# Attention scores in one VectorE pass, heads in pairs on partition halves, and filler products in the norm waits

## The chip, the cores and the metric

The kernel runs on one core of a Trainium2 chip. The metric is the device time of one execution in microseconds, the median of several runs. Five engines work side by side and meet only at semaphores: TensorE (PE; its weight loads are listed as PEld), VectorE (DVE), ScalarE (ACT), GpSimd (POOL) and SyncE (SP), which issues the weight loads.

## The reference

Two transformer blocks on 512 tokens of width 1024, all in float32. The first has two layers: SwiGLU feed-forward, a mixer, another feed-forward, each behind a residual and a layer norm, then `h + (p @ w_proj) * sigmoid(h @ w_gate)`. The mixer of layer 0 is a short convolution beside a state-space model. That of layer 1 is an attention of 8 heads of width 128 over 2 key heads, in which every query sees the 128 best keys by an index score. The second block is an RMS norm, an attention with 8 heads in three branches and 8 sliding-window heads with sinks, and a mixture of experts. What the change touches is the scores and their softmax:

```python
# compressed, selected and window branch; slopes are those of ALiBi, d = 64
s = einsum(q, k) * d ** -0.5
s = s - slope * dist
p = masked_softmax(s, mask)          # row maximum, exp, sum, divide
o = g0 * (p_cmp @ v) + g1 * (p_slc @ v) + g2 * (p_win @ v)
# sliding heads: window 128, the sink takes part in the maximum and in the sum
m = maximum(max(s), sink); z = sum(exp(s - m)) + exp(sink - m)
```

The norms are `(x - mean) * rsqrt(var + eps) * g + b` and `x * rsqrt(mean(x * x) + eps) * g`, over the 1024 features, which lie on the partitions in 8 chunks.

## The kernel before

Activations lie transposed, features on the partitions and 512 tokens in the free dimension. Weights come through a ring of six blocks of 1 MB that SyncE fills in the order of use. TensorE's results go into eight PSUM banks. A planner (`g`, class `Groups`) hands them out at build time: `hold` or `add` gives a label the next bank in turn (or the one named), and with it what must have been read before TensorE may write there. The order of work on each engine is written out by hand in one program per engine, and every engine works in order.

**Attention.** Class `Attention` serves both attentions as a list of items. An item is one head and one block `b` of 128 queries (b = 0 to 3). In the first attention (`att_c`, head width 128) an item has one branch with (b+1) x 128 keys. In the second (`att_n`, head width 64) tiles 0 to 3 have three branches: compressed (31 keys), window (128, 256, 384, 384 keys) and selected (128, 256, 384, 512); the first two share a bank, group 0, the third is group 1. Tiles 4 to 7 have one sliding branch (128, 256, 256, 256). A tile holds two heads, `kv` 0 on partitions 0 to 63 and `kv` 1 on 64 to 127; all four blocks of one are done, then those of the other. Both have 32 items per part: 32, and 32 + 32.

The items pass through a pipeline written out per step i:

- TensorE: scores of item i+1 (L1634), transposes of the weighted probabilities of i-2 (L1644, recorded under the helper's line L505), values times probabilities of i-3 (L1656, into half a bank at head width 64).
- VectorE: for item i the sum of the scores and the distances per branch (L1691, or L1693 with the slope), a maximum per branch (L1701), for sinks L1704, then the negated maximum (L1706); for item i-1 the factor 1/z (L1712 or L1714, L1716, and L1720 times the branch gate); for i-2 the copy of the transposes out of PSUM, when (group + item) is odd (L1671).
- ScalarE: exponentials with row sums for i (L1736), the other copies of i-2 (L1673), and after block 3 the head's output (L1893, L2115).
- POOL: probabilities times factor, one pass per branch (L1752).

Scores and transposes take turns on banks 0 to 5, outputs on 6 and 7. A matmul in float32 is recorded as two passes (two MATMUL and two LDWEIGHTS records), a transpose as one.

**Norms.** `tensor_stats` folds the sums and the squares of the chunks onto few partitions (L578), then spreads the mean to all (L585); VectorE makes the variance, ScalarE the root, VectorE the reciprocal (L650), and `tensor_scales` spreads that (L585 again). VectorE then subtracts and multiplies chunk by chunk (L631, L657), ScalarE applies gain and bias (L668), and the next product starts with the first chunk. In the norms "ffn1" and "ffn3" eight projections stand beside this (L469), four between the two spreads, four behind the second, and then the gate's products (L478); their banks are the next eight in turn, so that of projection 6 is the one of the spread mean. ScalarE copies projections 0 to 3 before its eight norm steps and 4 to 7 behind them (L1078).

## Time and profile before

| | us |
|---|---|
| median of 3 runs | 3364.46 (3362.58 to 3366.96) |
| the profiled execution | 3364.31 |
| its span in the trace | 3362.5 |
| TensorE busy | 3136.2 (93%) |
| VectorE busy | 1392.2 (41%) |
| ScalarE busy | 471.0 (14%) |
| POOL busy | 316.2 (9%) |
| mean granted clock of TensorE | 0.963 |

The page gives the busy time of each engine and the chain of work that ended last, followed back from the last instruction. The trace behind it can be asked by window, by line and in order of time. Matmuls are pipelined, so their durations overlap; the time from start to start tells more. A granted clock of 1.00 is TensorE's 2.4 GHz level, 0.50 its 1.2 GHz level. Line numbers are those of the kernel before.

### The profile page before, as it was taken

The numbers are of one execution on the slowest core, as the hardware profiler recorded it, in microseconds if no ns is written. First come the engines' busy times: TensorE is split into PE (matmuls) and PEld (weight loads), VectorE is DVE, ScalarE is ACT, GpSimd is POOL, SyncE is SP. The second block draws the span as 40 slices with busy tenths as digits, with TensorE's granted clock in tenths as the row PEclk, the third lists the DMA queues.
The fourth block names the chain that finished last, engine by engine and source line by source line (L and its number), as shares of the span: only waits on it lengthen the run. The fifth ranks groups of instructions, "written<-read, shape, count | busy, mean of one in ns | idle before, by whom it ended". The sixth has DMA issues, their size and how long they took to land.

```text
span 3362.5 us, 31721 instructions
## 1 busy us (share of the span) xinstructions
PE 3136.2 (93%) x12846; PEld 2170.7 (65%) x12846; DVE 1392.2 (41%) x3041; ACT 471.0 (14%) x1020; POOL 316.2 (9%) x304
## 2 busy tenths in 40 slices
PE   9999999889999999999997999999899989997774
PEld 7886446738888858888643478888365654453221
DVE  6563212426553426553558365543321780121112
ACT  1101010011000110010122210000211550011001
POOL 0000100110000100001012300001001550011010
PEclk9999998799999999999998999999999999988998
DMA  5222212012222212222121122222122001226997
GB/s 196 87 76 81 94 75 75 13 63 82 88 88 88 88 63 101 88 87 89 54 75 38 38 94 88 86 90 88 63 100 113 1 1 63 75 88 251 373 396 299
DMA packets 54200, 344.34 MB, mean 102 GB/s; under 512 B 7968, under 2 KB 8096, under 8 KB 15520
## 3 DMA queue, kind: packets, MB, share of 16 engines
q1 hardware_dynamic: 44352, 318.79, 25.4%
q10 hardware_dynamic: 5088, 15.05, 1.2%
q0 software_dynamic: 4608, 8.40, 0.7%
q8 instruction: 105, 1.72, 0.2%
q14 instruction: 47, 0.39, 0.0%
HBM read 335.92 MB, written 14.68 MB: 104 GB/s over the span
## 4 chain that ended last, share of the span: by engine, by line
PE 84%; DVE 7%; DMA 6%; POOL 1%; issue 1%; ACT 1%; SPq 1%; ACTq 0%; DVEq 0%; POOLq 0%
PE bank L777 44%; PE bank L469 24%; DMA ring<-in_weights 6%; PE bank L478 4%; PE bank L2427 2%; PE bank L1412 2%; PE bank L499 1%; PE bank L505 1%; POOL area L1752 1%; PE bank L1634 1%; PE bank L1656 1%; PE bank L1439 1%; DVE stat L1701 1%; DVE area L1946 1%; PE bank L585 1%
## 5 line engine op out<-in xcount | busy, mean ns | idle before, releaser
L469 PE MATMUL bank<-area,ring 128*128 128x512 f32 (+1 forms) x1220 | 452.4, 532 | 33.4 <-DVE area L1542 15.6
L469 PEld LDWEIGHTS bank<-area,ring 128*128 128x128 f32 x1220 | 213.8, 193 | 267.5 <-issue 231.1
L777 PE MATMUL bank<-buf_a,mixed 128*128 128x256 f32 x1408 | 320.2, 380 | 0.0
L777 PE MATMUL bank<-buf_b,mixed 128*128 128x256 f32 x1408 | 319.2, 379 | 0.0
L777 PEld LDWEIGHTS bank<-buf_a,mixed 128*128 128x128 f32 x1408 | 268.0, 190 | 36.7 <-DVE mixed L807 0.4
L777 PEld LDWEIGHTS bank<-buf_b,mixed 128*128 128x128 f32 x1408 | 267.6, 190 | 36.3
L469 PE MATMUL bank<-buf_b,ring 128*128 128x512 f32 x656 | 285.1, 593 | 0.7 <-ACT area L2115 0.7
L799 DVE TENSOR_TENSOR mixed<-ring 128x512 f32<-128x512 f32 (+1 forms) x124 | 84.1, 678 | 466.5 <-PE bank L777 460.0
L777 PE MATMUL bank<-buf_a,ring 128*128 128x256 f32 x1056 | 246.3, 383 | 9.1 <-DMA buf_a<-in_x 7.3
L777 PE MATMUL bank<-buf_b,ring 128*128 128x256 f32 x1056 | 245.3, 382 | 1.8 <-ACT buf_b L668 1.8
L777 PE MATMUL bank<-area,mixed 128*128 128x256 f32 x1056 | 233.8, 379 | 0.0
L777 PEld LDWEIGHTS bank<-buf_a,ring 128*128 128x128 f32 x1056 | 202.6, 192 | 37.2 <-DMA ring<-in_weights 7.3
L469 PEld LDWEIGHTS bank<-buf_b,ring 128*128 128x128 f32 x656 | 124.4, 190 | 156.6 <-issue 154.9
L777 PEld LDWEIGHTS bank<-buf_b,ring 128*128 128x128 f32 x1056 | 202.7, 192 | 30.5 <-issue 2.5
L777 PEld LDWEIGHTS bank<-area,mixed 128*128 128x128 f32 x1056 | 200.7, 190 | 27.2
L2427 PE MATMUL bank<-ring,area 128*64 128x512 f32 x512 | 139.6, 621 | 46.4 <-DMA ring<-in_weights 46.3
L777 PE MATMUL bank<-area,ring 128*128 128x256 f32 x792 | 176.8, 379 | 0.0
L1752 POOL TENSOR_SCALAR area<-area,stat 128x384 f32<-128x384 f32 (+3 forms) x160 | 138.3, 877 | 280.6 <-DVE stat L1720 205.9
L777 PEld LDWEIGHTS bank<-area,ring 128*128 128x128 f32 x792 | 150.5, 190 | 20.4
L2427 PEld LDWEIGHTS bank<-ring,area 128*64 128x64 f32 x512 | 39.9, 141 | 140.8 <-DMA ring<-in_weights 69.8
L505 PE MATMUL bank<-const,area 128*128 128x128 f32 x512 | 86.9, 296 | 37.4 <-POOL area L1752 29.7
L505 PEld LDWEIGHTS bank<-const,area 128*128 128x128 f32 x512 | 57.9, 147 | 89.8 <-issue 46.9
(351 smaller groups left out, 3275.2 us busy)
## 6 DMA issues: line engine op xcount, KB each, us to landing
ring<-in_weights SPq DMA_DIRECT2D x300, 1024.0 KB, 4.8
area<-chosen SPq DMA_DIRECT2D x8, 512.0 KB, 6.9
buf_a<-in_x ACTq DMA_DIRECT2D x4, 512.0 KB, 7.7
turn_tables<-area ACTq DMA_DIRECT2D x4, 512.0 KB, 2.6
area<-turn_tables ACTq DMA_DIRECT2D x4, 512.0 KB, 4.7
tokens<-area ACTq DMA_DIRECT2D x4, 512.0 KB, 3.5
out<-area ACTq DMA_DIRECT2D x4, 512.0 KB, 2.6
const<-in_const ACTq DMA_DIRECT2D x1, 1498.0 KB, 13.4
```

Of the source, the lines that this page charges most:

```text
L469: mm = pe.e.matmul(bank[0:w.shape[1], 0:n], w, x[k], start=k == 0, stop=k == len(pieces) - 1)
L478: mm = pe.e.matmul(bank[0:w.shape[1], :], w, x[k], start=k == 0, stop=k == len(x) - 1)
L499: mm = pe.e.matmul(out[b][:, 0:width], x[k][:, b * P:(b + 1) * P], w, start=k == 0, stop=k == len(x) - 1)
L505: return pe.e.transpose(out, in_, C("ident")[0:n, 0:n])
L585: mm = pe.e.matmul(out[:, b * P:(b + 1) * P], C("ident", 32 * b, 32 * b + 1).to_broadcast([P, P]), src, start=True, stop=True)
L777: mm = pe.e.matmul(b, w[:, k * P:(k + 1) * P], x(INPUT_OF[p], unit.lo + k), start=(unit.key, BANK_OF[p]) not in begun, stop=unit.last and ...
L799: made = tt(unit.mix("S1"), unit.quarter("A21"), unit.quarter("A22"), ALU.add)
L1412: mm = pe.e.matmul(b[:, ct * NB:(ct + 1) * NB], b_turned[rows, k, part, ct, :], ab_u[rows, ct, k:T:STEPS], start=k == 0, stop=k == STEPS - 1)
L1439: mm = pe.e.matmul(out[:, :, k], c_power[:, k, part, ct * PPC + i, :], ab_ends[i % 2][:, part, ct, 0:NB], start=False, stop=True, skip_gro ...
L1634: mm = pe.e.matmul(b[:, br["at"]:br["at"] + br["n"]], br["q"], br["k"], start=True, stop=True)
L1752: made = po.e.tensor_scalar(l, l, item["zs"][:, j:j + 1], None, ALU.mult)
L2427: mm = pe.e.matmul(out[rows, :], x, w, start=k == 0, stop=k == KD - 1)
```

## The change

- VectorE makes each branch in one instruction, `tensor_tensor_reduce`: (distance + score) times slope, and the running maximum into one column, starting from -1e20 or from the sink. For this the queries are scaled by d ** -0.5 / slope (a new constant `q_scale`, one value per partition and tile).
- Items of the second attention go in batches of two: both heads of a tile for the same block. The small passes (negated maximum, 1/z, gate) are one per batch, over adjacent columns of the statistics. On TensorE the score matmuls and the values matmuls of the two heads alternate, and both outputs lie in the two halves of one bank, evacuated at once (8 evacuations instead of 16). The first attention keeps batches of one.
- TensorE's order in a step is now scores, values, transposes. Banks are named: first attention 0 to 2 for scores, 3 to 5 for transposes, 6 and 7 for outputs; second attention 0 to 3, 4 to 6, and 7.
- In the second attention VectorE copies group 0 of the even item of each batch, ScalarE the rest. Slots for probabilities are 6 + 6 instead of 4 + 4, for transposes 8 instead of 5.
- In the norms without projections beside them TensorE does products whose result nobody reads: 6 behind the spread of the mean, 6 behind the second spread, for the RMS norms 6 behind the folds and 3 behind the spread. They write into the bank of the squares, after it was read.
- In "ffn1" and "ffn3" the projections' banks are chosen so that none is that of a spread: the second spread takes the fourth bank in turn, the projections cycle over the last four and the first two.

```diff
+    BESIDE, IDLE_ROOT, IDLE_SCALE, IDLE_RMS = ("ffn1", "ffn3"), 6, 6, 3
...
+        order = [(g.turn + j) % 8 for j in range(8)]
...
+        others = itertools.cycle(order[4:] + order[:2])
+        for m in range(KD):
+            if m == KD // 2:
+                plan_scales(st, order[3])
+            beside(m, next(others))
+        g.turn = next(others)
...
+    def idle_products(pe, label, read, n):
+
+        pe.wait_ge(*read)
+        for _ in range(n):
+            pe.e.matmul(bank(label)[:, 0:P], C("ident"), C("mean"), start=True, stop=True)
...
+        if st not in BESIDE:
+            idle_products(pe, ("squares", st), (square_read, STATS[st] + 1), IDLE_ROOT)
...
+        if st not in BESIDE:
+            idle_products(pe, ("squares", st), (square_read, STATS[st] + 1), IDLE_RMS if st in RMS else IDLE_SCALE)
...
+        idle_products(pe, ("squares", st), (square_read, STATS[st] + 1), IDLE_ROOT)
...
+        def score_steps(self, batch):
+
+            for k, group in enumerate(self.items[batch[0]]["groups"] if batch else ()):
+                for j in range(len(group)):
+                    for i in batch:
+                        yield i, k, self.items[i]["groups"][k][j], j == len(group) - 1
...
+            for s in range(-1, len(self.batches) + 3):
+                for i in self.batch(s + 1):
+                    for sem_, value in self.items[i]["ready"]:
+                        pe.wait_ge(sem_, value)
+                for i, k, br, last in self.score_steps(self.batch(s + 1)):
+                    b = opened(pe, g, (self.name, "s", i, k))
+                    mm = pe.e.matmul(b[:, br["at"]:br["at"] + br["n"]], br["q"], br["k"], start=True, stop=True)
+                    if last:
+                        end(g, mm, (self.name, "s", i, k))
...
+                for j, steps in enumerate(zip(*lists)):
+                    for i, (out, w, p) in zip(self.batch(s - 3), steps):
+                        mm = pe.e.matmul(out, w, p, start=j == 0, stop=j == len(lists[0]) - 1)
+                        if j == len(lists[0]) - 1:
+                            end(g, mm, (self.name, "a", i))
+                for i in self.batch(s - 2):
...
+                            mm = transpose(pe, b[:, c:c + P], item["slot"][k][:, c:c + P])
...
-                            if br["slope"] is None:
-                                made = ve.e.tensor_tensor(l, br["far"], s, ALU.add)
-                            else:
-                                made = ve.e.scalar_tensor_tensor(l, br["far"], br["slope"], s, ALU.mult, ALU.add)
+                            raw = bank((self.name, "s", i, k))[:, br["at"]:br["at"] + br["n"]]
+                            j = next(parts)
+                            made = ve.e.tensor_tensor_reduce(out=l, in0=br["far"], in1=raw, scale=br["slope"],
+                                                             scalar=HELD if item["sink"] is None else item["sink"],
+                                                             op0=ALU.add, op1=ALU.max, accum_out=item["m"][:, j:j + 1])
...
-                    for j, (l, _) in enumerate(item["parts"]):
-                        ve.step(ve.e.tensor_reduce(m[:, j:j + 1], l, AX.X, ALU.max))
-                    ve.settle()
...
-                      [stat[:, 16 + 16 * i:32 + 16 * i] for i in range(8)])
+                      [stat[:, 16 + 16 * i:32 + 16 * i] for i in range(8)],
+                      1, lambda i, n: (n + i) % 2, ((0, 1, 2), (3, 4, 5), (6, 7)))
...
-    n_wide, n_packed = [sp_n.get(T) for _ in range(4)], [sp_n.get(T) for _ in range(4)]
-    n_turned = [sp_n.get(T) for _ in range(5)]
+    n_wide, n_packed = [sp_n.get(T) for _ in range(6)], [sp_n.get(T) for _ in range(6)]
+    n_turned = [sp_n.get(T) for _ in range(8)]
...
+                      2, lambda i, n: i % 2 == 0 and n == 0, ((0, 1, 2, 3), (4, 5, 6), (7,)))
+    N_EVACUATED = 8
...
-            ac.e.activation(n_q[:, j, :], bank(("q", j)), ACT.Copy, scale=float(BD ** -0.5)).then_inc(q_done, 1)
+            ac.e.activation(n_q[:, j, :], bank(("q", j)), ACT.Copy, scale=C("q_scale", j, j + 1)).then_inc(q_done, 1)
```

## Rows read from the trace of the kernel before

**Rows 1.** The page: busy time of TensorE, and the chain by engine.

```profile
PE 3136.2 (93%) x12846; PEld 2170.7 (65%) x12846; DVE 1392.2 (41%) x3041; ACT 471.0 (14%) x1020; POOL 316.2 (9%) x304
...
PE 84%; DVE 7%; DMA 6%; POOL 1%; issue 1%; ACT 1%; SPq 1%; ACTq 0%; DVEq 0%; POOLq 0%
```

**Rows 2.** Windows: length, busy us (count) of PE PEld DVE ACT POOL, clock, DMA.

```profile
1812.00:1884.00 72.00, 53.23 (x305) 38.65 (x306) 53.27 (x185) 29.35 (x88) 34.47 (x32) 0.91 0.00 1
2586.00:2716.00 130.00, 118.83 (x693) 87.45 (x693) 95.13 (x359) 65.87 (x233) 73.81 (x94) 0.92 0.03 9
2716.00:2779.00 63.00, 56.39 (x284) 34.62 (x285) 48.41 (x206) 34.00 (x121) 30.05 (x35) 0.95 0.00 1
```

**Rows 3.** Chain of the whole span: start us, us, what; two heads' same step.

```profile
2632.20 1.16 DVE area L1693 x3
...
2647.75 1.17 DVE area L1693 x3
```

**Rows 4.** Timeline of PE, 2632 to 2648: start, us, instruction, idle before.

```profile
2638.43 0.95 PE L505 MATMUL bank<-const,area 128*128 128x128 f32 x7 [1.02 <-POOL area L1752]
...
2643.28 1.74 PE L1656 MATMUL bank<-area 128*64 128x128 f32 x14
2644.95 1.99 PE L1634 MATMUL bank<-area 64*128 64x31 f32 x6
```

**Rows 5.** Timeline of PE in the sliding part, the same step twice.

```profile
2739.62 0.44 PE L505 MATMUL bank<-const,area 128*128 128x128 f32 x2 [0.56 <-POOL area L1752]
...
2746.26 0.44 PE L505 MATMUL bank<-const,area 128*128 128x128 f32 x2 [0.55 <-POOL area L1752]
```

**Rows 6.** Chain of the first attention, 1845 to 1854.

```profile
1845.88 1.25 POOL area L1752
...
1849.48 0.69 DVE area L1671
...
1853.53 1.25 POOL area L1752
```

**Rows 7.** Windows behind four of the norms ("ffn0", "ab", "c", "nsa").

```profile
446.40:453.00 6.60, 5.22 (x6) 2.18 (x7) 6.43 (x11) 4.06 (x5) 0.00 (x0) 0.50 0.04 12
757.00:763.60 6.60, 4.81 (x15) 4.01 (x16) 4.38 (x7) 2.44 (x3) 0.00 (x0) 0.50 0.01 2
...
1945.00:1954.90 9.90, 7.90 (x22) 6.47 (x23) 7.49 (x13) 4.26 (x6) 0.00 (x0) 0.50 0.06 23
...
3006.50:3023.00 16.50, 16.17 (x76) 16.20 (x77) 7.86 (x36) 1.14 (x2) 0.73 (x1) 0.50 0.08 18
```

**Rows 8.** Timeline of PE in the norm "ffn0": the two spreads.

```profile
442.13 1.16 PE L585 MATMUL bank<-area,const 128*128 128x128 f32 x8 [0.19 <-DVE area L639]
444.93 1.16 PE L585 MATMUL bank<-area,const 128*128 128x128 f32 x8 [1.64 <-DVE area L650]
```

**Rows 9.** Timeline of PE and of ACT in the norm "ffn1".

```profile
1182.11 6.12 PE L469 MATMUL bank<-area,ring 128*128 128x512 f32 x8 [5.92 <-DVE buf_b L631]
...
1183.53 1.06 ACT L1078 ACTIVATE area<-bank 128x512 f32<-128x512 f32 x2
```

**Rows 10.** Groups by form: VectorE's two passes, the scan, ScalarE's accumulator read.

```profile
L1693 DVE SCALAR_TENSOR_TENSOR area<-const,bank 128x384 f32<-128x384 f32 x24 | 12.5, 546 | 0.0
L1701 DVE TENSOR_REDUCE stat<-area 128x1 f32<-128x384 f32 x24 | 12.4, 543 | 0.0
...
L1518 DVE TENSOR_TENSOR_SCAN area<-stat,area 128x128 f32<-128x128 f32 x32 | 10.5, 401 | 0.1
...
L1736 ACT ACTIVATION_READ_ACCUMULATOR area<-area,stat 128x1 f32 x160 | 29.9, 187 | 0.0
```

**Rows 11.** Halves in turn: index scores by form; a product and experts in the chain.

```profile
L1853 PE MATMUL bank<-area 64*128 64x256 f32 x16 | 2.0, 389 | 2.9 <-DVE area L1918 2.9
...
1164.99 6.87 PE bank L469 x16
...
3075.61 3.66 PE bank L2427 x14
```

200 lines of the change are left out of this document (96 added, 104 removed).

## Prediction

> **What bounds the kernel now.** The page comes first: TensorE is busy for 93% of the span and carries 84% of the chain that ended last [rows 1]. Such an average hides the places where TensorE waits, so the table of windows comes next. It cuts out the first attention (32 items, 128-wide heads, 72 us), the second attention's part with compressed, window and selected branches (32 items, 130 us) and its sliding part (32 items, 63 us) [rows 2]. Then one steady cycle of each is read in the timelines.
>
> In the second attention's first part the cycle of four items (one head) is 15.55 us [rows 3]. Of it TensorE stands still for 1.0 us, waiting for POOL [rows 4]; the other 14.5 us are its own work. So this part is bound by TensorE, with VectorE (95 of 130 us) and POOL (74 of 130) behind [rows 2]. In the sliding part the cycle is 6.64 us [rows 5], and VectorE, busy for 48 us in 63 with the ramps at both ends in it, is nearly without a hole [rows 2]. In the first attention the cycle is 7.65 us and its chain is a ring: POOL weighs two items and TensorE turns the second, 3.60 us (1845.88 to 1849.48); VectorE copies it, adds and reduces two more items and makes the next factor, 4.05 us (to 1853.53), and POOL starts again [rows 6].
>
> The third place is the norms. After each of them the granted clock is 0.50, its 1.2 GHz level, for 6 to 16 us, and TensorE works at half speed in it [rows 7]. Before each such fall it had done short work only, a spread of 1.2 us with a hole of 1.64 us behind it [rows 8]. Around the two norms in front of sigmoid gates it also waits 5.9 us in the middle of the small projections [rows 9].
>
> The tail waits for weights (DMA 6% of the chain) [rows 1]. Its loads start behind the router, so the tail moves as a whole with whatever ends earlier before it; I found nothing there that takes a gain back.
>
> **The merged score pass.** It removes one of two equally long VectorE passes per branch: add 546 ns, reduce 543 ns at 384 columns [rows 10]. What the merged pass costs is not in the trace. The lower bound is one such pass (546 ns). The upper bound is a pass at half rate: the scan, the only operation here that carries a value along while it reads two inputs, takes 401 ns for only 128 columns [rows 10], and at that rate some 0.95 us for 384, where today's two take 1.09. I take one pass plus 0.1 us for bringing out the maximum: a running maximum is what the plain reduce makes at full rate, and ScalarE's separate read of an accumulator takes 187 ns [rows 10], about half of it behind its neighbour. The Trainium skill (VectorE: DVE Perf Modes, Two Vector instructions with no wait between them) states that an operation with an accumulator output is two instructions; no VectorE row here shows it, and with 187 ns for each the sum below would be some 3 us less of a gain.
>
> **First attention.** Batches of one item, so only the merged pass and the order change. From the ring go the reductions of items 2 and 3 (together 1.2 us by 543 ns at 384 columns and proportionally at 512), in come two outputs of 0.1: 7.65 - 1.2 + 0.2 = 6.65 us [rows 6, 10]. The new order puts the values of one item (6 passes at 0.12) ahead of the turns; most of that lies in POOL's time for the item to be turned. 1.0 us times 8 heads = 8 us. With the merged pass at half rate it is about 0; if TensorE alone were the limit (53 us busy in 32 items, some of it at half clock) about 13.
>
> **Second attention, TensorE's share.** Two heads on opposite halves of the partitions are now issued in turn. That such halves run side by side is in the trace. The index scores alternate between partitions 0-63 and 64-127: 16 passes of 256 columns were busy for 2.0 us at 389 ns each, so they start every 0.107 us, where a 512-column product starts every 0.43 and 256 columns would take 0.215 [rows 11]. Where outputs alternate between halves, the experts' 512-column passes, 14 of them start within 3.66 us, every 0.26 instead of 0.43 [rows 11]. Today the attention stays on one half, and 14 values passes take 1.67 us, 0.119 each [rows 4]. For a pair of items on average (item b has windows and selections of 128 to 512 columns): scores 12 passes, none under 0.107 us, those of 384 at 0.16, of 512 at 0.21, and 0.2 for the change-over: 1.75 us, now some 2.9 (1.92 us for one item with 31, 384 and 384 columns [rows 4]); values 23 passes x 0.119 x 0.26/0.43 = 1.65, now 2.7; turns 11.5 x 0.13 = 1.5, as now. Together 4.9 us a pair, 19.6 for two heads against 29 now.
>
> **What is late next.** The scores of a pair need four banks, and the new pool for scores has exactly four. So the scores of the next pair wait until VectorE has read those of this pair, and values and turns are queued behind them on TensorE. The ring, from the second head's compressed score on: rest of the scores 1.65, values 1.65, the first head's turns 0.4 + 0.15, VectorE's copy of them 0.5, the merged passes of the first head (compressed 0.13, window and selected 0.44 each, by 546 ns for 384 columns, three outputs 0.3) and of the second head's first group (0.57 + 0.2), 0.1 back to TensorE: 6.5 us a pair, 26 us for two heads against 31.1 [rows 3, 4, 10]. The other engines, by their busy time of 32 items [rows 2]: POOL 73.8 / 4 = 18.5; ScalarE 65.9 and about 6 more for the copies that move to it, 18; VectorE 95 less the reductions (34), half of the small passes (12) and six tenths of a copy load of 15, plus 10 for the outputs, 13 to 15. None reaches 26. Four times 5.1 = 20 us. Ends: 46 us gained at 19.6, and a loss (the rivals).
>
> **Sliding part.** Here four banks hold two pairs and the ring does not close. Per pair, by the busy times [rows 2]: ScalarE 34.0 / 16 = 2.1, POOL 30.1 / 16 = 1.9, VectorE two merged passes 1.05, three small passes 0.5, one copy 0.4 = 1.95, TensorE some 1.95. Four engines at about 2 do not mesh perfectly: 2.5 us a pair, 10 us for two heads against 13.3 [rows 5]. Four times 3.3 = 13 us. The two further clears of slots cost 0.3 us at the start; filling and draining stay as they are. Second attention: 33 us.
>
> **Fillers.** Six products of 128 columns are 12 passes, 1.43 us by the 0.119 of [rows 4]. They lie in the holes of 1.64 us and before the first normalised chunk [rows 8], so they cost nothing while the clock is full, and 1.2 us each where it is already half. They can give back half of TensorE's busy time at 0.50: 5.2, 4.8 and 7.9 us in three of the four layer norms without projections beside them, and the fourth is like the second: 2.6 + 2.4 + 3.9 + 2.4 = 11.3 us [rows 7]. In front of the second attention the clock falls before the folds, where no filler stands: about 0. Before the router 16.2 us are worked at 0.50 [rows 7]; with products 36 columns wide the clock may fall again there: 2.5 us out of 0 to 8. Sum 13.8, of which I take 12, as one norm may keep its fall. Ends: -3 (it falls all the same and the fillers delay) and 19.
>
> **Banks beside the sigmoid gates.** Projections 4 to 7 no longer wait for the bank of the spread means; they end 3.4 us after the second spread. The gate's first products then need projections 4 and 5 copied, which ScalarE does only after its eight norm steps: 1183.53 + 1.06 = 1184.6, where today the last projections run until 1182.11 + 6.12 = 1188.2 [rows 9]. So 3.5 us earlier, and about 4 in the twin; but the 5 us of idleness ahead will again lower the clock, now under the gate's products (the projections of today lost 2.4 to it): 1.5 us each, 3 us together (0 to 7.5).
>
> **The sum.** Span 3362.5, execution 3364.31, median of the runs 3364.46: they agree, and I work from 3364.3. 8 + 33 + 12 + 3 = 56: 3308 us.
>
> **Rivals.** (a) Everything meshes: the ring of a pair is shorter than drawn, 22 us for two heads (+16), fillers 19 (+7): about 3285. For it: TensorE's own work is only 19.6. Against it: the four banks. (b) The merged pass runs at half rate: first attention 0 instead of 8, the ring of a pair 1.0 us longer (16 of the 20 are lost), sliding 8 instead of 13: 3308 + 8 + 16 + 5 = 3337. For it: the scan [rows 10]; against it: the plain reduce. The Trainium skill (Vector Engine (DVE) Microarchitecture Reference, Points that are easy to get wrong) has a rule by which a pass with two SBUF sources that are not bf16 halves its rate, since no port is left for the accumulator; here one source lies in PSUM, and no run here shows the rule. (c) The halves do not overlap in this order, with weights loaded between every two passes: scores 2.9, values 2.7, ring 8.7 us a pair, 35 us for two heads, 16 us lost instead of 20 won: 3344. Against it: [rows 11]. (d) The other side: the four score banks decide. They put scores, values, turns and score passes in series, and above 7.8 us a pair (31.1 / 4) the part is slower than now. With a half-rate pass and no overlap it is 9.8 us: 32 us lost instead of 20 won, first attention 0, sliding 3 instead of 13: 3308 + 52 + 8 + 10 = 3378. (e) The fillers do nothing: 3308 + 12 = 3320, a matter of the forecast's own spread.
>
> **Numbers.** The forecast with its spread of sizes (3294 to 3323) 0.58, (a) 0.14, (b) 0.13, (c) 0.08, (d) 0.05, and 0.02 for small losses that leave it within 0.2%. About 0.2% (7 us) is what a measurement of this kernel can tell from no change. The range goes from 3280 to 3342. Faster by over 0.2%: 0.92; within: 0.03; slower: 0.05.
>
> **What would show it.** Right: one VectorE instruction per branch of 550 to 650 ns at 384 columns; about 26 us for two heads in the second attention, with TensorE waiting for VectorE at the scores; values passes starting every 0.07 us; a cycle of 6.6 us in the first attention; a clock of 1.00 through four layer norms; the gate's products some 3.5 us earlier behind the last fold. Wrong: merged passes of 900 ns, values passes still at 0.12, a clock of 0.50 over much of the second attention because TensorE waits more (each 10 us of it cost up to 5), or TensorE and VectorE waiting for ScalarE, which takes over copies.

## The result

The changed kernel takes 3278.8 us (median of four, 3273.7 to 3282.0), the kernel before 3365.7 us beside it. The ratio is 0.974 with a 95% interval of 0.972 to 0.976: 87 us less, where 56 were predicted. 3278.8 lies just below the range given (3280 to 3342). The direction was right, and so was the kind of almost every step; the size of one stage was not.

The page of the changed kernel, which answers to [rows 1]: busy time by engine, and the chain by engine.

```profile
PE 3074.3 (94%) x12978; PEld 2145.1 (65%) x12978; DVE 1312.4 (40%) x2883; ACT 467.6 (14%) x1028; POOL 315.4 (10%) x304
...
PE 85%; DMA 6%; DVE 6%; ACT 2%; issue 1%; SPq 1%; POOL 0%; ACTq 0%; DVEq 0%; POOLq 0%
```

The shares say almost nothing. 83 us went, and TensorE is as busy a share as before. The table of windows by stage says more: first attention, second attention's part with three branches, its sliding part, in the changed kernel (length, busy us and count of PE PEld DVE ACT POOL, clock, DMA), to be held against [rows 2].

```profile
1809.80:1870.90 61.10, 53.66 (x304) 37.61 (x304) 35.22 (x178) 28.07 (x88) 34.47 (x32) 0.97 0.00 1
2567.80:2666.80 99.00, 86.45 (x768) 65.37 (x770) 55.84 (x301) 71.69 (x264) 79.57 (x100) 0.95 0.03 12
2666.80:2699.30 32.50, 24.26 (x211) 15.21 (x212) 20.95 (x106) 23.75 (x97) 23.53 (x28) 1.00 0.00 1
```

Same work, 32 items in each row. In the second stage VectorE fell from 95 us to 56, TensorE from 119 to 86 in 99. No engine now fills the stage: after TensorE comes POOL, which nothing relieved, with 80 of 99.

Where the time went, by the same marks in the two traces (a stage of attention runs from its first score to its last values pass; the norms by the distance between the same TensorE instructions):

| place | before | after | gained | predicted |
|---|---|---|---|---|
| first attention | 66.6 | 61.0 | 5.7 | 8 |
| second, three branches | 140.3 | 98.9 | 41.4 | 20 |
| second, sliding part | 51.5 | 32.5 | 19.0 | 13 |
| six norms with fillers | | | 13.3 | 12 |
| banks beside the gates | | | 3.3 | 3 |

The rest is small: 0.7 us gained in the first 13 us of the program, 1.8 lost between "ffn0" and "ab", where the clock is at 0.50 at other moments than before, and some 1.5 gained in the tail and around the second attention. Almost all that was missed stands in the second attention: 60.4 us instead of 33. The experiments take that stage apart. Its length, and that of four stretches of two heads in each part (first values pass of one to that of the next), is the measure below. "Sum" is the whole stage, "fill" the time from its first score to its first values pass, and "at 0.50" how much of the stage had the granted clock at 0.50. All are from one profiled execution of each kernel.

| kernel | sum | fill | cycles, three branches | cycles, sliding | at 0.50 |
|---|---|---|---|---|---|
| before | 191.8 | 11.2 | 37.6 31.1 31.1 29.3 | 13.3 13.3 13.3 11.6 | 27 |
| merged pass alone (b1) | 173.4 | 9.1 | 36.6 29.0 29.0 25.7 | 11.5 11.5 11.5 9.5 | 17 |
| paired heads alone (e5) | 165.6 | 15.8 | 27.1 27.6 26.4 24.5 | 12.1 11.5 11.9 8.8 | 36 |
| all but the merged pass (e2) | 154.6 | 15.8 | 23.9 26.4 23.8 21.1 | 11.5 11.5 11.9 8.8 | 42 |
| all but halves in turn (e1) | 143.4 | 12.6 | 25.9 26.9 25.6 19.9 | 9.2 8.7 8.6 6.1 | 7 |
| changed | 131.4 | 12.6 | 22.8 23.3 22.5 17.7 | 9.1 8.7 8.6 6.1 | 10 |

The stage of the changed kernel recurs in two runs whose edits don't touch it: 131.6 us in e4 and in e6. In a third, e10, it was 135.6.

### The profile page after: what moved, and what is told of

Read it like the earlier page. It is cut to its first block, busy times and chain, and to the rows that moved or that the text cites. A ratio compares the mean times of both kernels' runs of the same rounds, so it can differ in the third digit from the quotient of the medians.

```text
span 3279.3 us, 31761 instructions
## 1 busy us (share of the span) xinstructions
PE 3074.3 (94%) x12978; PEld 2145.1 (65%) x12978; DVE 1312.4 (40%) x2883; ACT 467.6 (14%) x1028; POOL 315.4 (10%) x304
## 4 chain that ended last, share of the span: by engine, by line
PE 85%; DMA 6%; DVE 6%; ACT 2%; issue 1%; SPq 1%; POOL 0%; ACTq 0%; DVEq 0%; POOLq 0%
PE bank L805 45%; PE bank L472 24%; DMA ring<-in_weights 5%; PE bank L481 4%; PE bank L2471 2%; PE bank L1439 2%; PE bank L502 1%; PE bank L1691 1%; PE bank L508 1%; PE bank L1466 1%; DVE area L1736 1%; PE bank L1675 1%; DVE area L1988 1%; DVE area L1716 1%; DVE stat L1988 1%
## 5 line engine op out<-in xcount | busy, mean ns | idle before, releaser
L827 DVE TENSOR_TENSOR mixed<-ring 128x512 f32<-128x512 f32 (+1 forms) x124 | 84.1, 678 | 461.1 <-PE bank L805 454.6
L829 DVE TENSOR_TENSOR mixed<-ring 128x512 f32<-128x512 f32 (+1 forms) x124 | 84.1, 678 | 76.0 <-PE bank L805 76.0
L472 PE MATMUL bank<-buf_a,ring 128*128 128x512 f32 x256 | 110.2, 593 | 0.0
```

The costliest lines, as they stand in the source:

```text
L472: mm = pe.e.matmul(bank[0:w.shape[1], 0:n], w, x[k], start=k == 0, stop=k == len(pieces) - 1)
L827: made = tt(unit.mix("S1"), unit.quarter("A21"), unit.quarter("A22"), ALU.add)
L829: made = tt(unit.mix("S3"), unit.quarter("A11"), unit.quarter("A21"), ALU.subtract)
```

## The experiments

**e1, halves one after the other.**

```diff
-            for k, group in enumerate(self.items[batch[0]]["groups"] if batch else ()):
-                for j in range(len(group)):
-                    for i in batch:
-                        yield i, k, self.items[i]["groups"][k][j], j == len(group) - 1
+            for i in batch:
+                for k, group in enumerate(self.items[i]["groups"]):
+                    for j in range(len(group)):
+                        yield i, k, group[j], j == len(group) - 1
...
-                for j, steps in enumerate(zip(*lists)):
-                    for i, (out, w, p) in zip(self.batch(s - 3), steps):
+                for i, steps in zip(self.batch(s - 3), lists):
+                    for j, (out, w, p) in enumerate(steps):
```

> The changed kernel with one part undone: in the second attention TensorE makes one head's scores and then the other's, and one head's values and then the other's, instead of alternating the two halves pass by pass. Theory 'overlap' (alternate passes on the two halves run side by side): a values pass starts 0.12 us after the one before instead of 0.059, 46 of them per two heads with the three branches and 14 in the sliding part, so 2.8 and 0.8 us; the 24 score passes per two heads lose up to as much again; the cycle of two heads goes from 23.3 to 26 to 28 us, the stage is 14 to 25 us longer, and the first attention stays where it is. Rival 'the ring is VectorE's, TensorE has room': the cycle stays within 0.5 us of 23.3 and the stage within 3 us. If the granted clock at the stage's opening falls to 0.50 as it did before the change, the alternation is also what kept it up, and that adds up to 7 us.

3291.5 us, ratio 0.978 (0.976 to 0.980). The stage is 12.1 us longer, its cycles 25.6 to 26.9 instead of 22.5 to 23.3; a little under what was expected, and all of it in the part with three branches. The expectation had counted too few passes: two heads have 92 values passes with three branches (4 pairs of 23), not 46, and the same theory with 92 would have given 5.5 us a cycle where 2.8 was written. The sliding part stays to a tenth: TensorE has room there. The clock did not fall at the opening.

**e7, the values alone one after the other** (the second half of that diff).

> The changed kernel with the values of the second attention one head after the other, its scores still alternating. Both in turn cost 12.1 us. Theory 'the values are where the halves overlap' (0.059 us a pass for 0.12, 46 and 14 of them per two heads, 16 times... 4 cycles of each kind: 14 us of TensorE's time): 9 to 12 us longer. Rival 'the scores, whose waits for a bank sit there': 0 to 4 us longer.

Again 143.4 us, and 3288.3 us in all, 0.977 (0.975 to 0.978). So the values carry the whole of the 12.1 us, and taking the scores in turn as well adds nothing. That doesn't show that alternating scores is worth nothing: e1 also puts TensorE's scores into the order in which VectorE reads them. From 2590 to 2660 TensorE's matmuls wait 0.7 us for score banks in e1 (3 times), and 5.6 us in e7 (11 times), so a loss and a gain may cancel there. The view of the waits (engine, line, releaser: us in total, times, longest), e1 and then e7:

```profile
PE bank L1675 <- DVE stat L1736: 0.7, 3, 0.2
```

```profile
PE bank L1675 <- DVE stat L1736: 5.6, 11, 0.8
```

TensorE's timeline of one pair's values (start, us, instruction), first the changed kernel, then e7:

```profile
2631.69 1.31 PE L1691 MATMUL bank<-area 128*64 128x128 f32 x20
```

```profile
2636.85 2.02 PE L1691 MATMUL bank<-area 128*64 128x128 f32 x20
```

The same 20 passes. In turn one starts every 0.11 us, and only where the one head's list meets the other's do they overlap; alternating, two start within 0.01 us of each other, two every 0.11. Over the four pairs of a cycle (12, 20, 28 and 32 passes) the values take 5.9 us in the changed kernel, at full clock, and 9.4 in e7: 3.5 us, and the first three cycles are 3.2 to 3.7 us longer.

**e2, two passes again**, in both attentions.

```diff
-                            made = ve.e.tensor_tensor_reduce(out=l, in0=br["far"], in1=raw, scale=br["slope"],
...
+                            if self.name == "att_c":
+                                made = ve.e.tensor_tensor(l, br["far"], raw, ALU.add)
+                            else:
+                                made = ve.e.scalar_tensor_tensor(l, br["far"], br["slope"], raw, ALU.mult, ALU.add)
...
+                    for i in self.batch(s):
+                        for j, (l, _) in enumerate(self.items[i]["parts"]):
+                            ve.step(ve.e.tensor_reduce(self.items[i]["m"][:, j:j + 1], l, AX.X, ALU.max))
```

(the sink goes back into the maximum, and the queries' scale to what it was)

> The changed kernel with the merged VectorE pass undone in both attentions: one pass adds the distances (and slope), a second one takes the maximum, the small passes still once per two heads. Theory 'merged pass': each scan costs its 0.40 us on the path of the ring, 6 per pair of items; 16 pairs with three branches and 16 sliding ones with 2 each: 38 + 13 = 51 us at most, and the stage of the second attention is 35 to 51 us longer; the first attention is back to a cycle of 7.6 us or above. Rival 'overlap and small passes did it': VectorE's scans lie beside TensorE's work, and the second attention is 0 to 15 us longer.

3311.7 us, 0.984 (0.982 to 0.986). The second attention is 23.3 us longer, between the two expectations: of the 51 us of scans less than half is on the path. In the three-branch part the granted clock was also at 0.50 for some 24 us, against some 10 in the changed kernel, and in the sliding part for some 18 us against none, so not all of the 23 is the scans'. The first attention takes 67.9 us, 6.9 more than changed, and 1.2 more than the kernel before. That was a surprise, and e6 goes after it. VectorE's groups by form, in the changed kernel and then in e2:

```profile
L1736 DVE CUSTOM_DVE_ANT_0 area<-const,bank 128x384 f32<-128x384 f32 x24 | 12.6, 550 | 0.0
L1736 DVE DVE_READ_ACCUMULATOR2_ANT stat<- 128x1 f32 x96 | 8.0, 83 | 0.0
```

```profile
L1737 DVE SCALAR_TENSOR_TENSOR area<-const,bank 128x384 f32<-128x384 f32 x23 | 11.9, 547 | 0.0
L1748 DVE TENSOR_REDUCE stat<-area 128x1 f32<-128x384 f32 x22 | 11.3, 543 | 0.0
```

The merged pass takes 550 ns where the plain one takes 547, and the reduction's 543 are gone. The read of the accumulator is an instruction of its own, 83 ns, but it lies almost wholly under its neighbours: in the chain below it shows as pieces of 0.01 us.

**b1, the merged pass alone**, in the kernel before.

```diff
-                            if br["slope"] is None:
-                                made = ve.e.tensor_tensor(l, br["far"], s, ALU.add)
-                            else:
-                                made = ve.e.scalar_tensor_tensor(l, br["far"], br["slope"], s, ALU.mult, ALU.add)
+                            j = next(parts)
+                            made = ve.e.tensor_tensor_reduce(out=l, in0=br["far"], in1=s, scale=br["slope"],
+                                                             scalar=HELD if item["sink"] is None else item["sink"],
+                                                             op0=ALU.add, op1=ALU.max, accum_out=m[:, j:j + 1])
...
-                    for j, (l, _) in enumerate(item["parts"]):
-                        ve.step(ve.e.tensor_reduce(m[:, j:j + 1], l, AX.X, ALU.max))
```

> The kernel before with the merged VectorE pass alone put in (and the scale of the queries that it needs), everything else as it was. Theory 'the merged pass is worth its scan wherever VectorE is on the ring': the first attention 66.6 -> 59.7 us (by the 6.9 that undoing it cost), the second 191.8 -> 160 to 168. Rival 'it needs the pairing' (with one head at a time the latencies of the small passes decide): the second attention 178 to 190 us.

3331.6 us, 0.989 (0.987 to 0.990). The first attention falls to 57.8 us: the merged pass is worth 8.8 us there, and 18.4 in the second, which lies between the two expectations. Of a steady cycle with three branches it takes only 2.1 us (31.1 to 29.0): one head at a time, this part was TensorE's, as the prediction read it.

**e5, both parts undone** (the diffs of e1 and e2 together).

> The changed kernel with both parts undone at once, the alternation of the halves in the second attention (worth 12.1 us alone) and the merged pass in both (23.3 us alone); what is left of the change there are the small passes once per two heads and the two heads' items side by side. The stage took 131.4 us changed and 191.8 before. Theory 'the parts add': 131.4 + 12.1 + 23.3 = 167 us (164 to 170), and the remaining 25 us to before are the small passes and the pairing. Rival 'they overlap, each hides the other' (with the scans on VectorE, TensorE's order matters no more): 155 to 159 us. Rival 'each makes the other dearer' (by the clock or by a fuller ring): above 172 us.

165.6 us: the parts add. So pairing two heads, with neither other part, is worth 26.2 us: the largest of the three, and the one the prediction had not priced by itself. The clock blurs it (36 us at 0.50 in e5, 27 before); but the second and third cycles with three branches, which have no fall of the clock in either, went from 31.1 and 31.1 to 27.6 and 26.4. The next runs look for what in it that is.

**e8, the small passes once per head; e12, the same on the kernel of e5.**

```diff
-                    z = item["zs_all"]
+                    for i in self.batch(s - 1):
+                        one = self.items[i]
+                        z = one["zs"]
...
```

(the floor or sink, the inverse and the gate then work on one head's sums, and likewise the maximum's scale)

> The changed kernel, VectorE's small passes (the maximum's scale, the sum's floor or sink, the inverse, the gate) made once per head instead of once per pair, the pair's exponentials and weighting still waiting for the second head's. With both other parts undone the second attention is 165.6 us where it was 191.8, so the pairing is worth 26 us. Theory 'the small passes are that': four more of them per pair with the branches and three with the sliding window, each 0.17 to 0.2 us with the one before it to settle, 16 pairs of each kind: 10 to 20 us longer. Rival 'what pairing gives is the shorter chain of hand-overs (four score banks, two heads per step), not the small passes': 0 to 6 us longer. The first attention stays at 61.0.

> The kernel of e5 (paired heads, halves in turn, two VectorE passes), with the small passes made once per head as well. The second attention took 165.6 us in e5. Theory 'the small passes of a pair are the gain where VectorE is on the ring': 16 pairs with branches and 16 with the sliding window, four and three passes more of 0.17 to 0.2 us each: 175 to 186 us. Rival 'the gain is the step of two heads, in which one head's latency lies beside the other's work': 165 to 170 us, as the merged kernel lost 3.9 by this edit, most of it in a cycle in which the clock fell.

135.3 us for 131.4, and 168.4 for 165.6 (3288.5 and 3325.2 us in all). Most of e8's 3.9 is in two cycles into which the clock fell (24.6 us for 22.8, 9.8 for 8.6); the other six are within 0.6 of the changed kernel, and e12 too had more of its time at 0.50 than e5 (49 us for 36). But e8's profile is not typical: that execution took 3277.2 us, its other three 3288.2 to 3291.1. By the medians e8 is 9.7 us slower than the changed kernel, and no trace shows where, so there the small passes may cost up to 10 us. For the 26 us of the pairing e12 is the fitting test, and there stage and medians agree, 2.8 and 3.3 us. The small passes are a small part of the 26.

**e13, four banks for the scores, heads one at a time** (on b1).

```diff
-                        g.add((self.name, "s", i + 1, k), (self.logits_read, at))
+                        g.add((self.name, "s", i + 1, k), (self.logits_read, at), bank=next(scores) if own else None)
```

(and two banks, in turn, for the turned weights)

> The kernel before with the merged pass (b1: 173.4 us in the second attention) and, in that attention, fixed banks: four for the scores, two for the turns, where scores and turns went round six together. Heads are still taken one at a time. Theory 'the four banks for scores are what the pairing gives': 150 to 160 us. Rival 'the banks were not short with one head at a time': 170 to 178 us.

165.9 us, between the two, and a lesson in reading totals. The steady cycles are 29.0, 29.0 and 11.5, those of b1 to the hundredth. Of the 7.4 us 7.1 lie in the first long cycle (36.6 to 29.5), the rest in the fill. TensorE there (length, PE busy and count, clock, DMA), b1 and then e13, each from the same point of the stage:

```profile
2577.00:2587.00 10.00, 8.36 (x47) 1.00 0.31 105
2587.00:2604.00 17.00, 16.60 (x60) 0.52 0.01 1
```

```profile
2574.00:2584.00 10.00, 8.49 (x48) 1.00 0.28 105
2584.00:2601.00 17.00, 15.97 (x104) 1.00 0.01 1
```

The same work ahead, then 0.52 in one and 1.00 in the other. The medians of the two kernels are alike (3331.6 and 3330.4 us), and b1's profile is the slowest of its four executions (3338.2 us), so this 7 us belongs to the profiled execution, not to the banks. The banks were not short.

**e15, half of the copies on VectorE again** (three-branch part of the changed kernel).

```diff
-                      2, lambda i, n: i % 2 == 0 and n == 0, ((0, 1, 2, 3), (4, 5, 6), (7,)))
+                      2, lambda i, n: (i + n) % 2 == 0, ((0, 1, 2, 3), (4, 5, 6), (7,)))
```

> The changed kernel with half of the copies of turned weights on VectorE again in the part with three branches, as before the change, where it now has one in four (the sliding part keeps its half under both). Theory 'VectorE is on the ring and was relieved by the copies': one more copy of 0.69 us for a pair on it, 16 pairs: 131.4 -> 138 to 143 us. Rival 'ScalarE's queue is as much on the ring, so it only changes hands': 129 to 134 us.

145.2 us, 13.8 longer, and 3296.7 in all, 0.981 (0.979 to 0.984). The cycles are 27.4, 27.4 and 26.9. The view of the waits, about three cycles each, of the changed kernel and of e15:

```profile
ACT area L1776 <- DVE stat L1747: 13.3, 11, 2.0
POOL area L1793 <- DVE stat L1761: 11.5, 6, 2.4
...
PE bank L1675 <- DVE stat L1736: 5.7, 11, 0.8
```

```profile
ACT area L1776 <- DVE stat L1747: 27.3, 10, 3.1
POOL area L1793 <- DVE stat L1761: 24.0, 8, 4.6
...
PE bank L1675 <- DVE stat L1736: 15.8, 18, 1.4
```

All three other engines wait twice or thrice as long for VectorE. One copy more stands in its queue for each pair, and that one, of the last group, can only be made when TensorE has turned it, with the next pair's score passes queued behind it. The edit changes the number of copies and their place together; it doesn't tell the two apart. The clock is not behind it: 14 us at 0.50, against 10.

**e17, the copies moved alone, on b1.**

```diff
-                    if (n + i) % 2:
+                    if (n + i) % 2 if len(item["groups"]) == 1 else n == 0 and i % 2 == 0:
```

> The kernel before with the merged pass (b1: second attention 173.4 us, with the clock up 166 as in e13; cycle of two heads 29.0 us) and one in four of the copies of turned weights on VectorE in the part with three branches, where it was one in two. Theory 'VectorE's copies were on the path in any order': the cycle 29.0 -> 25 to 27 us, the stage 8 to 14 us shorter at the same clock. Rival 'only with two heads a step': with one head at a time VectorE has room after the merged pass, and the cycle stays at 28 to 30 us.

The steady cycle is 29.0 us, to the hundredth that of b1; the stage's 168.4 differs from 173.4 by the opening's clock alone. So the copies matter only with two heads a step, as far as these two kernels show. One at a time TensorE's own work filled the cycle and VectorE's copies had room; paired, the ring runs through VectorE.

**e3, VectorE reads the banks in TensorE's order**, the first group of both heads, then the second of both.

```diff
-                for i in self.batch(s):
-                    item = self.items[i]
...
-                    for k, group in enumerate(item["groups"]):
+                for k in range(len(self.items[self.batch(s)[0]]["groups"]) if self.batch(s) else 0):
+                    for i in self.batch(s):
+                        item = self.items[i]
+                        group = item["groups"][k]
```

> The changed kernel, VectorE reading the four score banks in the order in which TensorE fills them (first group of both heads, then second of both), where it now reads both groups of one head and then both of the other. Theory 'the score banks decide the ring': TensorE's waits for a bank at the second head's scores (0.35 to 0.79 us in each pair of items) go, 16 pairs by about 0.5: 5 to 8 us off the second attention, its cycle 23.3 -> 21.5 to 22. Rival 'they only move to the next link' (exponentials, copies, VectorE itself): within 2 us of the changed kernel.

128.4 us; cycles 21.7, 22.2 and 20.2, within or below what was expected. The stage is only 3.0 us shorter, as the last cycle was 0.6 longer and one of the sliding part met a fall of the clock (9.7 us for 8.6). Both stages had 10.2 us at 0.50 in all, so the 3.0 is not the clock's. 3274.3 us in all.

**e14, five banks for the scores, on e11; four in the first attention.**

```diff
-                      1, lambda i, n: (n + i) % 2, ((0, 1, 2), (3, 4, 5), (6, 7)))
+                      1, lambda i, n: (n + i) % 2, ((0, 1, 2, 3), (4, 5), (6, 7)))
...
-                      2, lambda i, n: i % 2 == 0 and n == 0, ((0, 1, 2, 3), (4, 5, 6), (7,)))
+                      2, lambda i, n: i % 2 == 0 and n == 0, ((0, 1, 2, 3, 4), (5, 6), (7,)))
```

> The kernel of e11 (scores read in TensorE's order; first attention in its old order) with five banks for the scores and two for the turns in the second attention in place of four and three, and four and two in the first in place of three and three. Theory 'the score banks still hold TensorE back': second attention 128.3 -> 120 to 125 us. Rival 'with the reading order mended the turns' banks are as short, or VectorE sets the pace': 127 to 135 us. First attention: 58.7 -> 57.5 to 58.7 us, between the one that shared six banks (57.8) and itself.

Second attention 135.1 us, with cycles of 22.0, 22.2, 23.0: no better than e11. The theory is refuted; the fifth bank for scores takes one from the turns. 3278.2 us in all.

**e6, the old order in the first attention.**

```diff
+                if self.name == "att_c":
+                    self.tensor_turns(pe, s)
                 lists = []
...
+                if self.name == "att_c":
+                    for i in self.batch(s - 2):
+                        self.copy_turned(ac, i, False)
                 for i in self.batch(s - 3)[-1:]:
```

> The changed kernel, in the first attention alone TensorE's order scores, turns, values and ScalarE's order copy, evacuation, as in the kernel before, where the change put the values ahead of the turns and the evacuation ahead of the copy. The merged pass taken back left this stage at 67.9 us where the kernel before had 66.6, so something else of the change costs it 1.2. Theory 'the order': 61.0 -> 59.5 to 60 us. Rival 'the fixed pools of three, three and two banks in place of six in turn': stays within 0.4 us of 61.0.

58.7 us: 2.3 less, more than expected. The waits of the first attention, changed kernel, then e6:

```profile
PEld bank L1691 <- DVE area L1716: 8.9, 14, 0.8
PEld bank L1691 <- ACT area L1718: 5.4, 9, 0.8
PE bank L1691 <- ACT area L1718: 5.2, 8, 0.9
PEld bank L1691 <- ACT area L1935: 5.1, 6, 1.1
```

```profile
PEld bank L508 <- POOL area L1806: 12.9, 21, 1.0
PE bank L508 <- POOL area L1806: 4.3, 10, 0.8
```

With values ahead of turns TensorE waits at the values (L1691) for copies that VectorE makes (L1716) and that ScalarE makes (L1718) behind its evacuation (L1935). With turns first those waits vanish and only POOL's weighting is waited for. The steady cycle of a head is 7.11 us in the changed kernel and 6.64 in e6, which over the seven cycles that follow the fill is 3.3 us; the stage shows 2.3, because the last stretch of e6 has 3.4 us at 0.50 and that of the changed kernel none. In b1 the cycle is 6.64 too, so the order accounts for all that the changed kernel's cycle has more than b1's. 3277.4 us in all.

**e9, idle products at the opening of the kernel before.**

```diff
+                if self.name == "att_n" and i < 6:
+                    for _ in range(3):
+                        pe.e.matmul(banks[6][:, 0:P], C("ident"), C("mean"), start=True, stop=True)
```

> The kernel before with three idle TensorE products of 128 columns after the scores in each of the first seven steps of the second attention, nothing else. Before, the granted clock was 0.50 from 2593 to 2613 of the profile, 6 us after the attention's first score, and the first cycle of two heads took some 7 us more than the next. Theory 'it fell for TensorE's waits there, and costs 7 us': the clock stays at 1.00 and the stage goes from 191.8 to 184 to 186 us. Rival 'the products cost what the clock gives, or the clock falls all the same': 190 us or above.

3372.6 us, ratio 1.000 (0.999 to 1.002), and the stage 199.4 us: longer, not shorter. The profiled execution took 3375.7 us, and eight others lie between 3359.1 and 3378.0; where the clock fell in the shorter ones isn't known. In the profile the opening was cured, and the clock fell three times later, for 10, 10 and 7 us. The stage begins at 2582.4 there. Windows of TensorE in e9, the opening and the first two falls:

```profile
2594.00:2614.00 20.00, 18.48 (x120) 1.00 0.00 1
2678.00:2688.00 10.00, 10.00 (x37) 0.50 0.00 1
2698.00:2709.00 11.00, 11.00 (x44) 0.53 0.01 2
```

The first long cycle went from 37.6 to 33.0 us, the third and fourth from 31.1 and 29.3 to 36.0 and 35.7.

**e4, no fillers** (all three counts set to zero).

> The changed kernel without its idle TensorE products in the norms. Theory 'fillers keep the clock up': the passes behind the statistics run at granted clock 0.50 again and the time is 8 to 12 us longer, each norm with fillers by 1.4 to 3.3 us, ffn1 and ffn3 (which have none) by nothing. Rival 'fillers do nothing, the other edits moved the norms': within 2 us. The second attention stays at its length under both, unless the clock in its opening hangs on the norm ahead of it.

3292.5 us, 0.978 (0.977 to 0.980): 13.8 us. Windows of TensorE behind "ffn0", "ab", "ffn2" and "c" in the changed kernel (three of them in [rows 7] before the change), then the same four in e4:

```profile
446.00:453.00 7.00, 6.64 (x21) 1.00 0.01 2
757.00:763.00 6.00, 5.55 (x34) 1.00 0.00 0
1644.00:1651.00 7.00, 6.55 (x26) 1.00 0.00 0
1936.00:1943.00 7.00, 6.55 (x33) 1.00 0.00 0
```

```profile
446.00:453.00 7.00, 5.83 (x14) 1.00 0.01 5
757.00:763.00 6.00, 4.21 (x14) 0.50 0.01 3
1648.00:1655.00 7.00, 5.21 (x12) 0.61 0.00 0
1942.00:1949.00 7.00, 5.21 (x18) 0.64 0.00 0
```

Behind "ffn0" the clock stayed up in e4 without fillers, so that one gain (2.6 us by the marks) is not all theirs in every execution. Behind the other three the clock is lower in e4, as the theory says.

**e10, the banks beside the gates as before** (the planner's three functions for the norms and the per-layer projections).

> The changed kernel with the banks beside the gates of the per-layer inputs (in the two norms that have such products) taken in the order of the kernel before. Theory 'they are worth what the marks moved by there': 3.3 us longer in all, 1.3 at the first and 2.1 at the second. Rival 'the marks moved for another reason, the scales' bank is free anyway': within 1 us.

From the second spread of "ffn1" to the first of "ffn2" 0.7 us more, from the second of "ffn3" to the one of "ple1" 2.3 more: 3.0, as expected. In TensorE's timeline the wait of 5.92 us in the middle of the projections is back:

```profile
1167.23 3.60 PE L472 MATMUL bank<-area,ring 128*128 128x512 f32 x8
1176.76 5.58 PE L472 MATMUL bank<-area,ring 128*128 128x512 f32 x8 [5.92 <-DVE buf_b L648]
```

In the changed kernel all 16 run together, and the gate's product starts at 1181.88, 6.2 us earlier than before the change: 13.2 us behind the second spread instead of 16.4. The whole is 3285.7 us, 7 more. Most of what goes beyond the 3.0 stands in the second attention, which this edit doesn't touch: 135.6 us instead of 131.4, with two falls of the clock in its opening (3 and 7 us at 0.50) and one at its end. So 4 us between two single profiles of that stage can be the clock alone.

**e11 and e16, the parts that gained.** e11 is e3 and e6 together; e16 adds the first attention's four score banks.

> The changed kernel with the two edits that gained alone: VectorE reads the score banks in TensorE's order in the second attention (128.4 us instead of 131.4), and the first attention keeps the order of TensorE and ScalarE of before (58.7 instead of 61.0). Theory 'they add': 5.3 us less than the changed kernel, 3273 to 3274 us where the changed one has 3278.8. Rival 'later stages give it back (clock, weights' transfers)': 3276 to 3279 us.

> The kernel of e11 (reading order in the second attention, old order in the first) with four score banks and two turn banks in the first attention, as in e14, where it took 57.7 us against 58.7. Theory 'it adds': first attention 57.7, second 128.3, in all 3271 to 3272 us against 3278.8 of the changed kernel. Rival 'the clock's phases take it back': 3274 to 3279.

3272.3 and 3272.9 us, ratios 0.972 (0.970 to 0.974) and 0.972 (0.971 to 0.974). The second attention is as expected in both, 128.3 and 128.2, but the first in e16 is 58.7 us, like e11's: the 57.7 of e14 didn't come back. e11 and e16 have the clock at 0.50 for 3 us at that stage's end and e14 has not, and the steady cycle is 6.64 us in all three; the fourth score bank is worth nothing. Against the changed kernel's 3278.8 both are 6 us less. The intervals overlap; what carries the claim is that the two stage lengths recur in each of three profiles (58.7, 58.7, 58.7 and 128.4, 128.3, 128.2).

## Why the prediction was off

The step that failed is the ring of a pair, 6.5 us, and in it the merged passes with their outputs: 2.08 us in the sum, 1.38 in the trace. Added to it, the sum left the second attention's opening and its ends as they were, and both came out shorter.

**Merged pass.** Right in kind: one pass at full rate. The trace has two instructions for each branch, 96 passes and 96 reads of the accumulator. The Trainium skill (VectorE: DVE Perf Modes, Two Vector instructions with no wait between them) says that an operation with an accumulator output is two instructions; the trace agrees. What was wrong is the price of the second one. I charged 0.1 us an output on a path; from the start of a pass to the start of the next it adds 0.01. Five in the ring of a pair: 0.45 us of the 6.5. The passes themselves lie closer than I had them, too: at 384 columns one takes 550 ns, but the next starts 0.47 us after its start. Rival (b) is excluded by 550 ns. The rule of the Trainium skill named beside it (Vector Engine (DVE) Microarchitecture Reference, Points that are easy to get wrong), on two SBUF sources, was not tested: one source is in PSUM in every run. The prediction's "some 3 us" for outputs of 187 ns was too small by its own ring: 0.087 us more for five outputs in 16 pairs is 7 us in this stage alone.

**The ring of a pair.** Drawn right. The chain of the changed kernel goes through exactly the links named, from scores to values, turns, copy, score passes and back. One turn of it, at full clock (start us, us, what):

```profile
2630.41 1.35 PE bank L1675 x8
2631.76 1.24 PE bank L1691 x20
2633.01 0.60 PE bank L508 x4
2633.61 0.02 issue
2633.63 0.69 DVE area L1716
2634.32 0.09 DVE area L1736
2634.41 0.01 DVE stat L1736
...
2635.55 0.02 DVE stat L1736
2635.57 0.04 issue
2635.61 1.78 PE bank L1675 x9
```

Summed over the four turns of one cycle, and divided by four:

| link, us a pair | predicted | changed kernel | the same in e4 |
|---|---|---|---|
| rest of the scores | 1.65 | 1.61 | 1.55 |
| values | 1.65 | 1.58 | 1.43 |
| turns | 0.55 | 0.61 | 0.52 |
| copy | 0.5 | 0.59 | 0.59 |
| merged passes and outputs | 2.08 | 1.38 | 1.38 |
| handing over | 0.1 | 0.06 | 0.07 |
| sum | 6.5 | 5.83 | 5.54 |

The cycle taken in the changed kernel (2607.1 to 2630.4) has 3.4 us at 0.50 in it, at the shortest values and turns; the second cycle of e4, where this part is untouched, has none and takes 22.2 us. So the term that was mis-sized is the merged passes: 0.7 us a pair too dear, 0.45 of it for the outputs. The values gave 0.2 more at full clock: I had taken 0.61 as the factor of the overlap from outputs that alternate, and it is 0.5 (two passes every 0.11 us). Turns and copy cost a little more than I had. Against a steady 31.1 the cycles of 22.5 to 23.3 are 8.2 us less and not 5.1: 12 us over four, 11 of them the merged passes'. Three rows of the table make up the rest of the part's 21: the opening, 6.5 us; the last cycle, where the sliding part's short scores already stand behind the values (3.4); and a fill 1.4 longer.

**The opening.** The sum takes 5.1 us off each of four cycles and says nothing of the first, which was 6.5 us longer than the next. The profile of before had the clock at 0.50 for 20 us there, that of the changed kernel at 1.00. b1 against e13, e9 and e10 show that this moves between executions and edits that have nothing to do with it; these 6.5 us are in the 83, and no run shows that the change earns them.

**Sliding part.** "Four engines at about 2 do not mesh perfectly: 2.5 us a pair": it was 2.2. I kept fill and drain as they were; the drain shrank with the cycle (11.6 to 6.1). Here the merged pass alone gives 7.4 us, pairing alone 7.3, and both 18.9. The windows of the sliding part in b1 and in e5 show why (PE, PEld, DVE, ACT, POOL, clock):

```profile
2712.00:2744.00 32.00, 32.00 (x162) 18.51 (x160) 22.33 (x124) 22.15 (x83) 18.63 (x22) 1.00 0.01 1
```

```profile
2697.00:2730.00 33.00, 23.77 (x158) 14.45 (x158) 27.36 (x116) 20.98 (x86) 19.63 (x24) 0.79 0.00 1
```

With the merged pass alone TensorE is busy throughout; with the pairing alone VectorE is for 27 of 33 us, and the clock is down for part of it. That fits two bounds that stood close together, of which each part takes away one; it is read from busy shares, and the clock has a share in e5's figure that no run separates.

**What I should have asked** is what is left in the ring if a term is taken at its lower bound. Rival (a), the one with everything meshing, had 22 us for two heads and got a chance of 0.14, "Against it: the four banks". But the banks were already in the ring that I had drawn; what made it long was a price for which no row stood. The steady cycle came out at (a)'s. That the total lies near (a)'s 3285 too is partly luck: the fillers gave 13.8 and not its 19, and the opening and the sliding part made up for it.

**First attention.** The merged pass gave 8.8 us alone (8 predicted). The step that failed here is "most of that lies in POOL's time": values ahead of the turns, and the evacuation ahead of the copy, cost 2.3 (e6), 3.3 at the same clock, and the cycle came to 7.11 us, not 6.65. In the old order it is 6.64 (b1, e6). That it meets the 6.65 so well is in part luck, since the two outputs in it were charged 0.1 each and add 0.01.

**Fillers.** 13.8 us by the medians of e4; 12 predicted. Between the two profiles it is 9.9: e4 is 13.5 us behind after the router's norm and gets 3.6 of that back in the tail. By the marks 2.6, 1.5, 2.4 and 2.9 us in the four layer norms (2.6, 2.4, 2.4 and 3.9 predicted), 2.4 at the router as said, and 1.4 at "ple1", where I had nothing; 1.8 us were lost again by the clock in the stage ahead of "ab".

**Banks beside the gates.** 3.3 by the marks, 3.0 by e10; 3 predicted. The gate's product did come some 3 us earlier behind the second spread, and the clock fell beneath it as feared: 0.77 from 1181.8 to 1190, and 0.81 from 2359 to 2370 in the twin.

**Rivals (c), (d), (e)** are refuted. The values overlap completely, and the fillers work. Rival (d) names the ring that the trace shows, but it takes 5.8 us a pair, where only above 7.8 it would have lost. Rival (c), no overlap, gave 35 us for two heads; e1 measured 25.6 to 26.9. Its share for the values, 1.05 us a pair, is there: 3.5 us a cycle by the timeline, 3.2 to 3.7 in the cycle. Its share for the scores, 1.15, is not seen in e1, where the better order of the banks may hide it.

Two sums of the prediction are off without bearing on the outcome: VectorE's share for two heads adds up to 12.5 us, not 13 to 15 (it measured 14), and the chances for a faster kernel add up to 0.93, not 0.92.

What stays open: why the granted clock falls at the second attention's opening in one execution and not in the next. Why the pairing by itself gives 26 is narrowed, not closed: 14 us hang on the number and place of the copies once the merged pass is there too (e15), some 3 on the small passes (e12), some 7 on the opening's clock. What else came with the pairing has no run of its own: values ahead of turns in the second attention, the additional slots, and one evacuation for both heads.

## What to carry to other kernels

When engines hand work round in a ring, write down each link once with its lower bound and once with its upper, and give the chances over the two sums; one link taken 0.7 us a pair too dear cost this forecast 11 us, and it hid the rival that came. Judge an edit by its steady cycle, not by the stage or the total: two kernels with cycles equal to the hundredth differed by 7 us in the stage, by one fall of the clock. And which engine makes a copy may be worth nothing until the ring runs through that engine: a copy more or less for each pair was worth 0 us a cycle in the kernel before with the merged pass, and 13.8 us in the stage of the changed one.

## What the runs showed of the hardware

- VectorE's merged pass (add, scale, running maximum, one source in PSUM) has the rate of the plain one: 550 ns for 547 at 384 columns, and the next pass starts 0.47 us after its start. The accumulator's read takes 83 ns and adds 0.01 to the chain.
- Values passes that alternate between the two halves of the output start in twos: 20 in 1.31 us, against 2.02 in turn.
- Idle products kept the granted clock at 1.00 (2.4 GHz) behind three norms where it is 0.50 to 0.64 without them, but at the opening of the second attention they only moved the fall: in e9's profile it came 96, 116 and 137 us behind the stage's first score instead of 7.
- The clock also stayed at 1.00 where TensorE waited more. In the changed kernel's opening (length, PE busy and count, clock):

```profile
2565.00:2575.00 10.00, 7.78 (x57) 1.00 0.27 105
2575.00:2602.00 27.00, 23.04 (x206) 1.00 0.01 2
```

It is less busy here than b1 was in the 10 us before its fall (8.36).
